# Products of token tile 0 placed between the transposes of the two token tiles, behind three norms of a two-block transformer kernel

## The reference, cut to what matters

```
# first block
h = rmsnorm(x, mix_norm_g);  proj = h @ w_in
# each of the two layers of the second block
x = _layernorm(DEEPNORM_ALPHA * x + FFN_RES * _swiglu(x, ffn1_w_in, ffn1_w_out), ln1_g, ln1_b)
mix = _hybrid_mixer(x, ...)       # begins with  h @ w_mix_in
```

## Time and profile before

| | before |
|---|---|
| median of 3 runs | 2230.96 us (2226.61 to 2234.68) |
| the profiled execution's own time | 2233.84 us |
| its span in the trace | 2232.1 us |
| mean granted clock of TensorE | 0.974 of full speed |
| TensorE matmul busy | 2135.5 us, 96% of the span |
| VectorE busy | 1393.9 us, 62% |
| ScalarE busy | 1096.1 us, 49% |

### The profile page before, as it was taken

How to read it: one execution, slowest core, us unless ns; L and a number is a source line. 1 busy time by engine, 2 the same in 40 slices (tenths; PEclk the granted TensorE clock), 3 DMA queues, 4 the chain that set the end, 5 groups by cost and what they waited for, 6 DMA issues and landing times. The chain is left out here.

```text
span 2232.1 us, 35886 instructions
## 1 busy us (share of the span) xinstructions
PE 2135.5 (96%) x14491; PEld 1931.0 (87%) x14491; DVE 1393.9 (62%) x2044; ACT 1096.1 (49%) x1707; POOL 84.1 (4%) x132
## 2 busy tenths in 40 slices
PE   6999899999989999999989998998999999998998
PEld 5788799899868889888979978986888988897996
DVE  6765688555556685566665555555668556666554
ACT  4576466444334587356334433433458635543442
POOL 1200000000000002200000000000000220000000
PEclk9999999999999899999989998999999999998999
DMA  6433455555645344333445554564544433344553
GB/s 244 162 114 118 157 189 186 185 169 177 213 150 189 118 133 146 114 131 103 163 133 188 206 186 137 169 221 144 187 132 133 136 124 118 114 163 140 188 207 113
DMA packets 271629, 351.56 MB, mean 158 GB/s; under 512 B 9891, under 2 KB 225549, under 8 KB 271501
## 3 DMA queue, kind: packets, MB, share of 16 engines
q1 hardware_dynamic: 271501, 349.75, 46.7%
HBM read 348.68 MB, written 1.05 MB: 157 GB/s over the span
## 5 line engine op out<-in xcount | busy, mean ns | idle before, releaser
L1514 DVE TENSOR_TENSOR ring_r<-ring,ring_hi 128x1024 fp32r<-128x1024 f32 x642 | 780.9, 1224 | 543.5 <-ACT ring_hi L1111 542.2
L1111 ACT ACTIVATE ring_hi<-ring 128x1024 fp32r<-128x1024 f32 x642 | 675.5, 1058 | 768.8 <-PE ps L651 721.4
L649 PE MATMUL ps<-xT_hi,ring_hi 128*128 128x256 f32 x2912 | 833.8, 286 | 7.8 <-issue 7.8
L650 PE MATMUL ps<-xT_r,ring_hi 128*128 128x256 f32 x2912 | 821.8, 282 | 0.0
L651 PE MATMUL ps<-xT_hi,ring_r 128*128 128x256 f32 x2912 | 821.7, 282 | 0.0
L649 PEld LDWEIGHTS ps<-xT_hi,ring_hi 128*128 128x128 f32 x2912 | 554.7, 190 | 23.1 <-issue 17.9
L650 PEld LDWEIGHTS ps<-xT_r,ring_hi 128*128 128x128 f32 x2912 | 554.6, 190 | 0.1
L651 PEld LDWEIGHTS ps<-xT_hi,ring_r 128*128 128x128 f32 x2912 | 554.1, 190 | 0.0
L651 PE MATMUL ps<-ring_hi,tok_r 128*128 128x512 f32 x536 | 212.8, 397 | 0.0
L649 PE MATMUL ps<-ring_hi,xT_hi 128*128 128x512 f32 x432 | 177.2, 410 | 3.4 <-DVE tok_r L1514 1.5
L649 PE MATMUL ps<-ring_hi,wide_r 128*128 128x512 f32 x440 | 173.3, 394 | 0.0
(11 more groups left out here) (269 smaller groups left out, 2415.6 us busy)
## 6 DMA issues: line engine op xcount, KB each, us to landing
ring<-in_w_mix_in SPq DMA_DIRECT2D x92, 1024.0 KB, 4.9
ring<-in_ffn_w_in SPq DMA_DIRECT2D x88, 1024.0 KB, 5.0
ring<-in_ffn_w_out SPq DMA_DIRECT2D x44, 1024.0 KB, 4.8
ring<-in_w_branch SPq DMA_DIRECT2D x24, 1024.0 KB, 5.2
ring<-in_w_in SPq DMA_DIRECT2D x22, 1024.0 KB, 5.1
ring<-in_w_ffn_up SPq DMA_DIRECT2D x22, 1024.0 KB, 5.0
ring<-in_w_ffn_down SPq DMA_DIRECT2D x11, 1024.0 KB, 4.8
ring<-in_w_mix_out SPq DMA_DIRECT2D x8, 1024.0 KB, 4.9
```

The lines of the kernel that those rows point to most:

```text
L649: pe.matmul(out_, stat[0], mov[0], start=first, stop=False)
L650: pe.matmul(out_, stat[0], mov[1], start=False, stop=False)
L1111: act.activation(half_of(ring_hi[:, s % HIGHS, :], s, q), half_of(ring[:, s % SLOTS, :], s, q), ACT.Copy).then_inc(w_hi, 1)
L1514: return dve.tensor_tensor(lo, whole, hi.bitcast(F32), ALU.subtract)
```

## The change

`norm` gets a function to call behind the transposes of each token tile. Behind the three norms named above it calls `opening`, which issues tile product h0 t0 between the transposes of tile 0 and those of tile 1, and behind the latter the other three, in the order h1 t0, h0 t1, h1 t1. The wait for the drained banks moves along to the front of `opening`. The other norms and chunks keep their order. No instruction is added or taken away on any engine, and the lists of the other engines are the same.

```
-            def by_tiles(L, c, h, s):
+            def one_tile(L, c, h, t):
+                s = c.slots[h]
                 act, w = acts[c.act], block(s, BANK)
...
+                if t == 0:
+                    for q in range(HALVES):
+                        wait_block(L, s, q)
+                if c.event is not None:
+                    wait_xT(c.event if L is None else norm_event(L, 0), t, h)
+                for k in range(4):
+                    mm = product(bank(2 * c.pair + t), [a[:, 4 * h + k, t * P:(t + 1) * P] for a in act], [v[:, k, :] for v in w],
+                                 h == 0 and k == 0, h == 1 and k == 3)
+                    if t == T - 1 and k % 2:
+                        used(mm, k // 2)
+                return mm
...
+            def opening(L, c, t):
+
+                if t == 0:
+                    for b, n in c.need.items():
+                        if n:
+                            pe.wait_ge(drained[b], lap(L, n, FREE_LAP[b]))
+                for h, tile in (((0, 0),) if t == 0 else ((1, 0), (0, 1), (1, 1))):
+                    one_tile(L, c, h, tile)
...
-            def norm(event, src, base=4):
+            def norm(event, src, base=4, then=None):
...
                         tr.then_inc(hat_turned, 1)
+                    if then:
+                        then(t)
...
-            norm(0, xhat)
+            norm(0, xhat, 4, lambda t: opening(None, head1[0], t))
...
-                norm(norm_event(L, 0), x, 0)
+                norm(norm_event(L, 0), x, 0, lambda t: opening(L, mix[0], t))
```

More of the change, by code:

```diff
@@ L655, in wait_xT, with by_tiles @@
                 pe.wait_ge(xT_dve, parts_of(event, t, g))
-            def by_tiles(L, c, h, s):
+            def one_tile(L, c, h, t):
+                s = c.slots[h]
                 act, w = acts[c.act], block(s, BANK)
[L660 to L671, removed]
+                if t == 0:
[9 more added lines that the diff above has]
+                return mm
+            def by_tiles(L, c, h):
+                one_tile(L, c, h, 0).then_inc(out_done, 1)
+                one_tile(L, c, h, 1)
+            def opening(L, c, t):
[5 more added lines that the diff above has]
+                    one_tile(L, c, h, tile)
             def half(L, c, h, q):
                 act = acts[c.act]
-                if h == 0 and q == 0:
+                if h == 0 and q == 0 and c.event is None:
                     for b, n in c.need.items():
@@ L680, in half @@
                 s = c.slots[h]
-                if c.event is not None or h == 1 and c.tail:
+                if c.event is not None:
+                    return
+                if h == 1 and c.tail:
                     if q == 0:
-                        by_tiles(L, c, h, s)
+                        by_tiles(L, c, h)
                     return
```

## The result

The changed kernel takes 2242.17 us (median of 4 runs, 2241.86 to 2245.21) against 2231.04 us (4 runs, 2226.61 to 2234.68): a ratio of 1.0054, with a 95% interval of 1.0034 to 1.0074. It is slower by 11.1 us between the medians; 9.3 us were forecast. The ratio beside it, with its 95% interval in brackets, is not taken from the medians, so the two can be up to 1 us apart.

The account below looks back on a forecast made before the run. The prediction took TensorE as the bound, with the second weight slot bounding the mixer's opening after the change. Layers +3.4 and +3.9 us and first block +2.0 sum to 9.3 us: 2230.96 + 9.3 = 2240.3 us, range 2233 to 2247.

Parts of the forecast that it names:

- The slot's readiness bounds the layer: Mixer's opening: h1 t0 must wait for the second weight slot, with TensorE idle about 4 us behind tile 1's transposes.
- a layer would win nothing even without slips: Layers: slot ready at 660.74 plus three tile products, 8.4 us, gives 669.14; the next chunk began at 669.13 before.
- The slip of the slot: First term, each layer: tile 1's transposes wait behind h0 t0, so the second slot is ready 1.2 to 1.9 us later; 1.4 taken.
- The upper bound of 2.5 us: Layers: the most the second slot would slip, if all of h0 t0 ran at half clock.
- The clock: Second term, each layer: half clock behind the idle of about 4 us costs 1.9 to 2.4 us; 2.0 taken.
- The first block: First block's norm: chunk 1.2 us later and VectorE's chain late, so the memory norm 2.0 us later; bounds 1.2 and 4.1.
- the layers' own term: Layers: h0 t0 runs 9 to 11 matmuls at 0.43 us, the rest at 0.233, ending at 656.8 to 657.2.
- the wait for slot 3: First block: slot 3's first half moves to 43.1, TensorE would want it at 42.8: some 0.4 us more.
- VectorE's chain: First block: tile 1's lows, angles, sine, table load and next split come 4.06 us later; 3.1 us left at 62.5.
- The sum: Whole kernel: 3.4 and 3.9 for the layers plus 2.0 for the block, 9.3 us; median 2240.3, 0.42% slower.
- The rival that the slips would be absorbed: Later stages: TensorE's waits on others shrink, so nothing measurable changes; about +1.5 us, 2232.5; chance 0.07.

Follow-up runs that it names:

- either repair: Layers only, against the change's order there: h0 t1 put ahead of h1 t0 (2231.46 us, 1.0000), or the second weight slot split earlier (2227.77 us, 0.9984).
- with the slot early: Change's order in the layers only, second weight slot split earlier on ScalarE and VectorE, first block old: 2227.77 us, 0.9984 against the kernel before.
- the run with the filled wait: Change's order in the layers only, plus 16 unread matmuls behind tile 1's transposes: 2235.65 us, 1.0012 against the kernel before.
- the layers alone: New order in the two layers only, first block in the old order: 2241.03 us, 1.0044 against the kernel before.
- The block with the clock brought up beforehand: New order in the first block only, plus 12 unread float32 matmuls ahead of its norm: 2234.36 us, 1.0012 against the kernel before.
- two parts of the change alone: New order in the first block only (2236.18 us, 1.0018) and in the two layers only (2241.03 us, 1.0044), each against the kernel before.
- the exchange: Layers only, h0 t0 in the gap as in the change, but h0 t1 ahead of h1 t0: 2231.46 us, 1.0000 against the kernel before.

## Why the prediction was right

**The slot's readiness bounds the layer.** Right, and shown: the wait was 4.12 us in both layers of two kernels (about 4 forecast), it ended with `ring_r`, and it went with either repair. That a layer would win nothing even without slips holds for the change's order; with the slot early the same tile product in the gap won 2.9 and 2.4 us.

**The slip of the slot.** The slot was ready at 662.08, where 662.1 was forecast, but 0.30 us of that is the later start of the whole stage, which the forecast did not have. From tile 0's first transpose on, the slot was ready after 12.77 us in both layers before, and after 13.81 and 14.21 us in the changed kernel (662.08 - 648.27, 1555.84 - 1541.63): slips of 1.0 and 1.4 us, where 1.4 was taken for both. The path was the one described: some 8 of 12 matmuls at half clock in the first layer and 9 to 10 in the second (9 to 11 forecast), tile 1's transposes 1.9 and 2.3 us late, a part given back by ScalarE. The upper bound of 2.5 us was nearly met in the run with the filled wait, 2.3 us.

**The clock.** 10.02 - 8.40 = 1.6 us a layer in the changed kernel and 10.77 - 8.40 = 2.4 us in the first layer of the layers alone; 2.0 was taken. The filled wait shows the cause. The Trainium skill, "TensorE: Matmul & The Clock Gate", Part 1, says that for modelling the ramp is under 1% of a typical span and that one should not fit a specific count of slow matmuls. The two terms here, 3.2 us of 2240, are under 1% too, but the change is itself 0.5%, and with them left out the forecast would have been 5.3 us and "no change", against 11.1 measured. The same part of the Trainium skill says that how many slow matmuls come is run-variable, and the runs agree: h0 t0 took 4.4 us in one execution and 5.2 us in another.

**The first block** was right in its mechanism, but three of its sizes were off. The step "h0 t0 starts at 24.35 instead of 24.69, takes 2.8 us, and the transposes start at 27.15" took the full clock for granted, where the layers' own term had h0 t0 at half clock; it took 4.45 us, and the transposes came at 28.91. The 1.57 us for these transposes are a row of weight loads at half clock; behind h0 t0 at full clock they took 29.70 - 28.91 = 0.79 us. So the chunk was 2.31 us late instead of 1.2, and the wait for slot 3 was 0.20 us instead of 0.4. VectorE's chain was 5.16 us late instead of 4.06, caught up 1.25 us instead of 0.93 (65.19 against 61.28 ahead of the memory norm is 3.91), and got back 1.04 us of the wait for ScalarE (1.13 forecast): the memory norm came 2.88 us late instead of 2.0. The block with the clock brought up beforehand gives 1.35 us, below the 2.0. That VectorE's chain is what carries the lateness on to the memory norm is read from its rows; no run took that chain apart from the rest.

**The sum.** 2.77 + 3.63 + 2.88 = 9.3 us in the three places of the trace, where 3.4 + 3.9 + 2.0 = 9.3 was forecast: the layers came out 0.9 smaller and the block 0.9 larger. That the two sums are the same to 0.1 us is luck, and the spans of this pair of traces differ by 8.0 us and not 9.3. The measured 11.1 us has an interval of 7.6 to 16.5 us, and no more than this can be said of the rest. The rival that the slips would be absorbed falls: two parts of the change alone each were slower than before beyond their intervals.

## What to carry to other kernels

Before work is moved into an idle gap, look up what each piece *behind* it needs, not only what the moved piece needs: here the gap was real and was filled, but the order of the three other pieces turned it into a wait of 4.1 us for an operand that used to be hidden by the piece now moved away. When such a wait appears, first exchange the waiting piece with one whose operands are ready, or bring the operand's preparation into the idle time of the engine that makes it; the exchange turned +0.44% into 0.00%, the latter into -0.16% with the same order of matmuls. Then look again at what bounds the stage: with the slot as the bound, a faster tile product ahead of it only became a wait of 1.56 us. Count moved matmuls at half clock if they start behind an idle stretch, and count half clock once more behind each new wait of about 4 us.

## What the runs showed of the hardware

A gap of 4.12 us cost TensorE 1.6 to 2.4 us beyond itself. In the changed kernel the fall came late: the granted clock was 1.00 over the whole wait (658 to 662 us) and 0.50 over 664 to 666. In the kernel with the layers alone it reads 0.56 over 660 to 662, inside the wait, and the cost was the larger one. Unread matmuls in the gap kept the clock up, and the 36 products behind it took 8.47 us instead of 10.02 to 10.77.

The granted clock reads 1.00 from the start of the trace on, also over 24 to 28 us of the changed kernel, while its matmuls from 24.46 on were 0.43 us apart, as at half clock; with unread matmuls ahead the same ones took 2.88 us for 12. At the start of these traces the spacing of matmuls is the better witness of the clock.

One and the same kernel spreads over 2222.9 to 2240.5 us, 0.8% (29 runs of the kernel before, beside the first set). The place of the clock's steps moves between executions: in eight layers of the old order the same 12 products took 3.52 to 4.80 us. Whether that makes the whole spread was not tried.
